# Two-block transformer kernel in float32 pairs: remainders of the weights written over the landed unit

## What is computed

```python
h = h + merged @ w_out[i]
h = h + swiglu(rms_norm(h, ffn_norm_g[i]), w_gate[i], w_up[i], w_down[i])
...
ys = jnp.stack([y_four, y_conv, y_gqa, y_diff], axis=2)
return jnp.sum(gates * ys, axis=2) @ lp["w_out"]
```

## Time and profile before

| | |
|---|---|
| median of 3 runs | 2769.59 us (2769.1 to 2772.91) |
| the profiled execution's own time | 2779.2 us |
| its span from the first to the last instruction | 2777.4 us |
| granted TensorE clock, mean | 0.907 of full speed |
| TensorE busy | 2383.8 us, 86% |
| VectorE busy | 1702.0 us, 61% |
| ScalarE busy | 1051.0 us, 38% |
| mean rate of the transfers | 140 GB/s |

### The profile page before, as it was taken

One profiled execution on the slowest core, in us unless ns is written; L12 is line 12 of the kernel. 1 busy time (PEld: TensorE's weight loads), 2 busy tenths in 40 slices (PEclk: granted clock), 3 DMA queues, 4 the chain that ended last, 5 costly groups with the idle time before them and its releaser, 6 DMA issues.

```text
span 2777.4 us, 42805 instructions
## 1 busy us (share of the span) xinstructions
PE 2383.8 (86%) x17529; PEld 2200.3 (79%) x17529; DVE 1702.0 (61%) x2085; ACT 1051.0 (38%) x1202; POOL 279.1 (10%) x277
## 2 busy tenths in 40 slices
PE   4766688979999978779999988679998998877998
PEld 4722378979999977679999877569998987657998
DVE  5589734545548775456556965555545786555554
ACT  4200233444334444334344444334334434433432
POOL 3857200020000001100000000200000001010000
PEclk8877778989999998689999988779999998978999
DMA  5267634425555442135555432124555442113552
GB/s 164 93 264 307 239 98 137 152 76 172 184 175 160 151 138 78 44 122 162 185 162 164 154 107 61 46 91 152 181 173 156 151 152 91 61 39 113 174 176 90
DMA packets 282994, 388.32 MB, mean 140 GB/s; under 512 B 7847, under 2 KB 255965, under 8 KB 276702
## 3 DMA queue, kind: packets, MB, share of 16 engines
q1 hardware_dynamic: 279148, 379.40, 41.8%
q10 hardware_dynamic: 3282, 5.74, 0.6%
q0 software_dynamic: 416, 1.08, 0.3%
HBM read 385.04 MB, written 1.05 MB: 139 GB/s over the span
## 4 chain that ended last, share of the span: by engine, by line
PE 68%; DVE 22%; issue 4%; ACT 4%; POOL 1%; DVEq 0%; SPq 0%; DMA 0%; ACTq 0%
PE L L733 56%; PE M L733 5%; DVE w_rest L349 3%; PE M L855 2%; DVE work L2093 2%; DVE m L1641 1%; POOL work_r L711 1%; DVE m L1897 1%; DVE gate L1897 1%; DVE work L2070 1%; DVE n_rest L1650 1%; ACT w_high L343 1%; DVE m L1712 1%; DVE gate L1706 1%; PE M L1098 1%
## 5 line engine op out<-in xcount | busy, mean ns | idle before, releaser
L733 PE MATMUL L<-n_high,w_high 128*128 128x256 f32 x3584 | 1052.7, 294 | 74.2 <-DVE n_rest L1683 22.7
L733 PE MATMUL L<-n_rest,w_high 128*128 128x256 f32 x3584 | 1035.7, 289 | 0.0
L733 PE MATMUL L<-n_high,w_rest 128*128 128x256 f32 x3584 | 1035.3, 289 | 0.0
L349 DVE TENSOR_TENSOR w_rest<-raw,w_high 128x2048 fp32r<-128x2048 f32 x311 | 712.8, 2294 | 374.5 <-PE L L733 339.1
L733 PEld LDWEIGHTS L<-n_high,w_high 128*128 128x128 f32 x3584 | 710.3, 198 | 98.0 <-issue 83.9
L343 ACT ACTIVATE w_high<-raw 128x2048 fp32r<-128x2048 f32 x311 | 593.9, 1911 | 502.1 <-PE L L733 424.4
L733 PEld LDWEIGHTS L<-n_rest,w_high 128*128 128x128 f32 x3584 | 711.2, 198 | 0.7
L733 PEld LDWEIGHTS L<-n_high,w_rest 128*128 128x128 f32 x3584 | 710.0, 198 | 0.0
L711 POOL TENSOR_TENSOR work_r<-kv,work_r 128x512 fp32r<-128x512 f32 (+2 forms) x44 | 64.4, 1466 | 2054.4 <-ACT work_r L1297 2054.4
L733 PE MATMUL M<-work_r 128*128 128x256 f32 (+3 forms) x744 | 175.2, 391 | 68.2 <-POOL work_r L711 33.1
L733 PEld LDWEIGHTS M<-work_r 64*128 64x128 f32 (+2 forms) x744 | 124.4, 219 | 105.7 <-issue 50.0
(11 more groups left out here) (341 smaller groups left out, 2907.9 us busy)
## 6 DMA issues: line engine op xcount, KB each, us to landing
raw<-in_w_in SPq DMA_DIRECT2D x116, 1024.0 KB, 5.5
raw<-in_w_ffn SPq DMA_DIRECT2D x99, 1024.0 KB, 5.2
raw<-in_w_ada SPq DMA_DIRECT2D x48, 1024.0 KB, 8.0
raw<-in_w_out SPq DMA_DIRECT2D x16, 1024.0 KB, 5.0
raw<-in_w_gate SPq DMA_DIRECT2D x11, 1024.0 KB, 5.3
raw<-in_w_up SPq DMA_DIRECT2D x11, 1024.0 KB, 5.3
raw<-in_w_down SPq DMA_DIRECT2D x11, 1024.0 KB, 4.9
raw<-in_w_four SPq DMA_DIRECT2D x6, 1024.0 KB, 5.0
```

The source lines that it names most:

```text
L349: nc.vector.tensor_tensor(w_rest[:, u.first % 2, :], raw[:, u.first % 4, :], w_high[:, u.first % 4, :].bitcast(F32), ALU.subtract).then_in ...
L733: ins = mm(dst, a, b, start=first and i == 0, stop=last and i == 2, skip_group_check=skip)
```

## The change

`w_rest` gets four slots, and they are the memory of `raw`: VectorE writes the remainder of a unit over the unit itself. The two slots of 2048 words of its own are gone, and `s5z`, which lay over them, lies elsewhere. VectorE makes `w_rest` of unit u+2 at its step for u, and no longer waits for `unit_done` in `split_rest`. At the two places where the row of units starts, it makes two remainders at once (`start_rest`). A slot of `raw` is now read by TensorE, so the transfer of unit u waits for `unit_done` of unit u-4 where it waited for `rest_ready` of unit u-4. Both halves of the heads' normalisation stand at step 2 of `gate3`.

```diff
-        raw = sb("raw", [P, RAW, UNIT])
-        w_high = sb("w_high", [P, RAW, UNIT], F32R)
         over = ExitStack()
         with over:
-            s5z = over.enter_context(nc.sbuf_tensor("s5z", [P, 4096], F32))
-        w_rest = sb("w_rest", [P, REST, UNIT], F32R)
+            raw = over.enter_context(nc.sbuf_tensor("raw", [P, RAW, UNIT], F32))
+        w_rest = sb("w_rest", [P, RAW, UNIT], F32R)
+        w_high = sb("w_high", [P, RAW, UNIT], F32R)
...
         def split_rest(dve, u):
             dve.wait_ge(high_ready, u.count(1))
-            if u.first >= 2:
-                dve.wait_ge(unit_done, u.count(-1))
-            nc.vector.tensor_tensor(w_rest[:, u.first % 2, :], raw[:, u.first % 4, :],
+            nc.vector.tensor_tensor(w_rest[:, u.first % 4, :], raw[:, u.first % 4, :],
                                     w_high[:, u.first % 4, :].bitcast(F32), ALU.subtract).then_inc(rest_ready, 1)
...
         def ahead_rest(dve, u, last):
-            if u.first + 1 < last:
-                split_rest(dve, u.plus(1))
+            if u.first + 2 < last:
+                split_rest(dve, u.plus(2))
+
+        def start_rest(dve, first):
+            for k in range(2):
+                split_rest(dve, Unit(first + k))
...
                     else:
-                        sp.wait_ge(rest_ready, u.count(-3))
+                        sp.wait_ge(unit_done, u.count(-3))
...
                 if a < 4:
-                    sp.wait_ge(rest_ready, v - 3)
+                    sp.wait_ge(unit_done, v - 3)
...
-            split_rest(dve, Unit(0))
+            start_rest(dve, 0)
...
-            split_rest(dve, Unit(BEFORE_ADA))
+            start_rest(dve, BEFORE_ADA)
...
-                gl(3, {2: lambda: head_normed(0), 3: heads_split}, start=BESIDE["diff"][1])
+                gl(3, {2: lambda: (head_normed(0), heads_split())}, start=BESIDE["diff"][1])
```

More of the change, by code:

```diff
@@ L49 @@
 RAW = 4
-REST = 2
 LAM_INIT = [0.8 - 0.6 * float(np.exp(-0.3 * l)) for l in range(LAYERS)]
@@ L197, in build @@
             s5w = over.enter_context(nc.sbuf_tensor("s5w", [P, 11264], F32))
+            s5z = over.enter_context(nc.sbuf_tensor("s5z", [P, 4096], F32))
         dft256 = work[:, 0:1024].rearrange("p (s l k) -> p s l k", s=2, l=2)
@@ L726, in parts @@
                 return [w[:, u.first % n, :].rearrange("p (k n) -> p k n", k=shape)
-                        for w, n in ((w_high, RAW), (w_rest, REST))]
+                        for w, n in ((w_high, RAW), (w_rest, RAW))]
             def product(dst, wh, wr, xh, xr, first, last, skip=False, weights_move=False):
```

## The result

The changed kernel takes 2828.98 us (median of 4 runs, 2826.51 to 2831.34) where the kernel before takes 2771.25 (4 runs beside it). The ratio is 1.0209, 95% interval 1.0197 to 1.0221: 57.7 us slower. The forecast was 2812, with a range of 2784 to 2836.

A forecast was written before the change was run, and what follows sets the result against it. TensorE was taken to bound each stage, with later transfers making ScalarE late at boundaries. Terms 19.3 + 7.3 + 7.7 + 11.7 + 3.3 - 6.9 gave +42.4 us on the median 2769.59: 2812 us, range 2784 to 2836.

The forecast's parts named there:

- the likeliest case: Whole kernel: late landings make ScalarE late, +42.4 us in sum, 2812 us, bounds 2798 to 2826; chance 0.65.
- the rival with the clock: Eleven lengthened TensorE waits also let its clock fall, 2 us each: 2834 us; chance 0.12.
- B: Five normalisations before `mem_q` and `ffn_up`: sum starts 2.05 us later, less 0.67 gained; net +1.45 each, +7.3 in all.
- C: Other stage boundaries, where a result goes from ScalarE to the next stage's operands: lateness not hidden, +7.7 us.
- D: The attentions: ScalarE's `w_high` waits for a landing with exponentials behind it, and entries into `diff` and `gqa`: +11.7 us.
- E: The start and the convolution's taps: one remainder more stands ahead of VectorE's work there, +3.3 us.
- A: Three normalisations beside `ffn_down`: `w_high` waits for landings ahead of squares and norm; +6.5 us each, +19.3 in all.
- The bound and the useless gain: Inside a stage TensorE bounds at 5.77 us a unit; removing VectorE's 339.1 us of waiting for it saves nothing.
- The step that decides: Transfers start when unit u-1 is done, so ScalarE's `w_high` makes it reach unit u's result 1.3 to 1.8 us late.
- F: The heads: a 2.29 us remainder leaves the path to `proj3` in each of three passes, -6.9 us.
- The milder rival: Transfers alone land 1 us sooner at 22 places, 2790 us, or more lateness is hidden, 2783 us; chance 0.10.

The follow-up runs named there:

- `w_high` two ahead: The changed kernel with ScalarE making `w_high` two units ahead instead of three, and in `gate3` `proj3`'s first ahead of the heads' copy: 2808.37 us, ratio 1.0132.
- mixed: The changed kernel with ScalarE making `w_high` two units ahead, but three ahead from `conv_u` to `proj1` of each full pass: 2772.48 us, ratio 1.0000.
- both gains: The kernel before with the heads in one step and the second unit's remainder ahead of the norm at `mem_q` and each `ffn_up`: 2756.46 us, ratio 0.9961.
- `w_high` last: The changed kernel with `w_high` still three units ahead but last in ScalarE's step in the ordinary stages: 2840.53 us, ratio 1.0251.
- both with the filler: The changed kernel with extra matmuls of constants ahead of five sums of squares: twenty gave 2834.64 us, ratio 1.0214; ten gave 2829.68 us, ratio 1.0210.

## Why the prediction came out as it did

The direction and the mechanism were right, and the size lay in the range: 57.7 us where 42.4 were forecast. But on the forecast's base, 2769.59, that is 2827, just past the 2798 to 2826 of the likeliest case and on the way to the 2834 of the rival with the clock; of the 15.3 us by which the forecast was short, B has 8.4, most of it the clock's, C, D and E together 5.4 and A 1.1. (The lower bound is loose as well: 8 and 10 less than 2812 make 2794, not 2798.)

- **The bound and the useless gain.** Right. VectorE's 339.1 us behind TensorE went, and bought nothing; the 22 units of an `ffn_up` still take 5.78 us each.
- **The step that decides.** Right. SyncE alone with the later wait gives the loss and more; ScalarE and VectorE each one unit nearer take it away while the transfers stay late. The lateness was 2.1 us at the end of `zu` (385.05 against 382.9), 1.8 forecast.
- **A.** Right: 6.5 forecast, 7.9, 6.5 and 6.1 measured. The last `w_high` was forecast at unit 9's end + 7.6 and ended at + 7.4; the first was the one with the slow sum. One sign was wrong by its own sum: "the wait before 846.60, 3.1 us now, is about 9.5" puts nearly all of the 6.5 there, though 2.8 of it stand ahead of unit 9; measured, TensorE waits 2.5 ahead of the sum and 6.5 at the next stage.
- **B, the term that was mis-sized.** "TensorE's sum, which began at 1244.04, needs the last squares [...]: start 1246.1, +2.05" and "Net +1.45, five times +7.3": measured 15.7. (The two figures themselves, 2.05 less 0.67, make 1.38, five times 6.9.) Where the clock held, the place cost 1.7; where it fell, 3.0 to 4.1. I had the fall of the clock as a rival of its own and gave it 0.12, as a thing that comes on top everywhere or nowhere. It came at five of eight gaps, 1.7 to 1.8 us each (5.41 against 3.6 to 3.7), some 9 us: four of them in B, some 7 of the 8.4 us that B was short, and one in A. My argument against it, that those waits "exist already", was wrong at the sums: there TensorE had not waited at all before, and had run straight on from the unit.
- **C, D, E.** 28.1 measured, 22.7 forecast; right in kind.
- **F.** -11.6 measured and -6.9 forecast, but 2.9 of that is c0's `diff` at another clock (above), so -8.7; the run with the heads alone gives -11, from -7 to -15. The remainder's own 2.2 us are in the trace (1185.62 to 1187.83 in the earlier trace rows). Most of what lies beyond it is in the first unit of `proj3`: with the heads alone it is 0.6, 0.2 and 0.65 us shorter in the three passes.
- **The base.** The rows come from a profiled execution that was 8 us slow, but the sum was added to the median, so this is not what the forecast was short by. It matters where two traces are compared: 7.6 us of its slowness lie at the two places named below the table and make F and the rest look better than they are. With them taken out the traces differ by 56.7 us, near the medians' 57.7. A third place can't be counted so. In the slow execution the stretch between the first and the second unit of c0's `gate3`, in `diff`, ran at half the clock. In the run with the heads alone, which is the same kernel up to there, it did not; but in the changed kernel it did, and took as long to the hundredth. Before, changed, and heads alone:

```profile
1118.87:1137.66 18.79, 17.51 (x71) 15.45 (x71) 8.60 (x21) 5.22 (x13) 3.46 (x2) 0.50 0.17 57
```

```profile
1147.30:1166.09 18.79, 17.51 (x72) 15.47 (x72) 8.61 (x21) 5.21 (x13) 3.46 (x2) 0.50 0.06 13
```

```profile
1119.07:1133.27 14.20, 11.70 (x71) 10.36 (x71) 8.07 (x20) 5.22 (x13) 3.45 (x2) 0.86 0.23 74
```

So these 4.6 us stand in both traces and in no row of the table. The other traces say on which side they belong. In the four others in which the eight sums begin without a gap (`w_high` two ahead, mixed, each engine one unit nearer, both gains) the stretch took 14.0 to 14.3 us; in the four others in which ScalarE stands three units ahead behind late landings (later transfers alone, `w_high` last, both with the filler) it took 15.8 to 18.8. The changed kernel's profiled execution is at its median, that of before is not at its own. That suggests a clock loss of 1.6 to 4.6 us which belongs to the change and which the slow base hid; with one trace of the kernel before it isn't shown, and it would have to be made up elsewhere, since the traces already agree with the medians to 1 us.

The milder rival was told that a transfer alone might land 1 us sooner, as the Trainium skill's fit for GpSimd's queue ("DMA: Bandwidth & Descriptors", "Anatomy of one DMA") gives. The medians stayed at 5.5 and 5.2 us; for SyncE's queue the measured rows hold, not that fit.

## What to carry to other kernels

A wait taken from an engine that only waited for the bottleneck gave nothing inside a stage; what counts is what the same edit does to the moment at which a buffer comes free. When buffers are merged, ask when the transfer can start now, how long it takes, and what stands in order behind the instruction that waits for the landing: here one unit's later start was 1.3 to 2 us of lateness, paid at the boundaries of stages and in the attentions. How far each engine works ahead belongs together: a later transfer asked for ScalarE one unit nearer, and that in turn for VectorE one unit nearer, or for ScalarE three ahead in the few stages where VectorE needs it. The first of these came out 6 us faster than the kernel before, the second level with it, both with the heads' gain in them.

## What the runs showed of the hardware

TensorE's units in `ffn_down` run at one of two rates, both at a granted clock of 1.00. Two stretches, of the kernel before and of the changed one, each inside the first block's `ffn_down`:

```profile
783.00:822.00 39.00, 39.00 (x334) 39.00 (x333) 16.05 (x7) 13.44 (x7) 0.00 (x0) 1.00 0.58 192
```

```profile
798.00:840.00 42.00, 42.00 (x373) 42.00 (x372) 17.76 (x8) 13.45 (x7) 0.00 (x0) 1.00 0.57 194
```

334 matmuls reach into the 39 us of the first, 373 into the 42 us of the second. By the starts of the units that is 5.65 and 5.44 us a unit. In all eleven traces each of the four `ffn_down` had one of these two values (the mean over its third to eighth unit), 15 of the 44 the slower one: two in the kernel before, three in the run with the later transfers alone and in the one with each engine one unit nearer, none in the changed kernel nor in the one with the heads alone. No pattern by kernel is seen. It is 2.3 us for a stage of eleven units. What sets it stays open.
